# A layer with expert lookup: query weights in sixteen steps of one row, V rows from dot 50, and six places for U from dot 48

## The reference

```python
h = rms_norm(x, norm2_g)
qc = (h @ w_query).reshape(T, 8, 2, 128)              # 8 heads, 2 halves
s = einsum('chpd,hpnd->chpn', qc, sub_keys)           # 128 keys a half
top_s, top_i = top_k(s, 16)                           # of both halves
cand_s, cand_i = all 16 x 16 sums of a pair, and 128 * i0 + i1
best_s, best_pos = top_k(cand_s, 16)                  # 16 experts a head
g = softmax(best_s)
act = gelu(einsum('chkd,cd->chk', expert_u[expert_idx], h))
out = x + einsum('chk,chkd->cd', g * act, expert_v[expert_idx])
```

## Time and profile before

| | |
|---|---|
| median of three runs | 1734.62 us (1733.67 to 1737.07) |
| profiled execution | 1737.77 us, its span 1735.9 us |
| VectorE busy | 1315.3 us, 76% |
| TensorE busy | 1300.8 us, 75% |
| GpSimd busy | 889.8 us, 51% |
| ScalarE busy | 413.4 us, 24% |
| DMA | 584.24 MB, 337 GB/s on average |
| granted TensorE clock | 0.852 of full speed |

### The profile page before, as it was taken

The page is one execution under the profiler, slowest core; times in us unless marked ns, Lnnn a source line. Parts: engine busy times, 40 slices in busy tenths (PEclk is TensorE's granted clock), DMA queues, the critical chain, the costliest instruction groups (busy, mean ns, idle before and its releaser), DMA issues.

```text
span 1735.9 us, 15043 instructions
## 1 busy us (share of the span) xinstructions
PE 1300.8 (75%) x4980; PEld 888.0 (51%) x4980; DVE 1315.3 (76%) x2030; ACT 413.4 (24%) x859; POOL 889.8 (51%) x546
## 2 busy tenths in 40 slices
PE   9999999999984552365556555566597999999950
PEld 7888887778883441122223323333265555555530
DVE  5554655556799999988889999898769665666678
ACT  5333443643110101001034433432054000000000
POOL 1000010000386887888888888888622733334365
PEclk9999999999997776566676788876597999999985
DMA  7886557158799999999999999999965999999998
GB/s 237 220 208 191 173 152 223 59 185 297 267 416 417 421 389 385 382 420 421 414 384 392 393 418 400 391 421 420 394 207 159 403 409 411 409 409 409 409 402 349
DMA packets 150233, 584.24 MB, mean 337 GB/s; under 512 B 15586, under 2 KB 28596, under 8 KB 117268
## 3 DMA queue, kind: packets, MB, share of 16 engines
q0 software_dynamic: 74384, 438.08, 63.2%
q1 hardware_dynamic: 75460, 144.37, 25.2%
q10 hardware_dynamic: 320, 0.93, 0.1%
HBM read 580.95 MB, written 2.36 MB: 336 GB/s over the span
## 4 chain that ended last, share of the span: by engine, by line
POOL 31%; PE 26%; DMA 19%; DVE 16%; issue 7%; ACT 1%; DVEq 0%; ACTq 0%; POOLq 0%
DMA v_rows<-in_peer_expert_v,pick_row 16%; POOL big L676 13%; POOL v_rows L656 11%; POOL more_rows L676 7%; PE ps L1664 6%; PE ps L1666 6%; PE ps L1665 6%; DVE big L1564 4%; DVE more_rows L1522 4%; DVE big L1522 3%; DMA more_rows<-in_peer_expert_u,pick_row 2%; PE ps L2066 1%; PE ps L2090 1%; DVE big L1544 1%; DMA big<-in_peer_expert_u,pick_row 1%
## 5 line engine op out<-in xcount | busy, mean ns | idle before, releaser
L656 POOL DMA_INDIRECT v_rows<-in_peer_expert_v,pick_row x256 | 354.0, 1383 | 292.6 <-DVE big L1564 208.8
L2066 PE MATMUL ps<-v_rows,diag 128*128 128x512 f32 (+1 forms) x480 | 284.8, 749 | 210.4 <-DMA v_rows<-in_peer_expert_v,pick_row 206.1
L1522 DVE CUSTOM_DVE_ANT_0 big<-big 128x2048 f32<-128x2048 f32 x154 | 351.0, 2287 | 45.6 <-DMA big<-in_peer_expert_u,pick_row 45.3
L1564 DVE SCALAR_TENSOR_TENSOR big<-v_rows,pick_w,big 128x1280 f32<-128x1280 f32 x175 | 271.6, 1552 | 130.7 <-DMA v_rows<-in_peer_expert_v,pick_row 126.2
L676 POOL DMA_INDIRECT big<-in_peer_expert_u,pick_row x154 | 299.1, 1942 | 49.2 <-issue 47.2
L2066 PEld LDWEIGHTS ps<-v_rows,diag 128*128 128x128 f32 x480 | 119.3, 265 | 361.9 <-DMA v_rows<-in_peer_expert_v,pick_row 236.0
L1003 DVE TENSOR_TENSOR split_lo<-raw,split_hi 128x1024 fp32r<-128x1024 f32 x119 | 145.8, 1225 | 145.0 <-ACT split_hi L704 119.4
L1522 DVE CUSTOM_DVE_ANT_0 more_rows<-more_rows,big 128x2048 f32<-128x2048 f32 x102 | 232.1, 2286 | 21.5 <-DMA more_rows<-in_peer_expert_u,pick_row 21.1
L676 POOL DMA_INDIRECT more_rows<-in_peer_expert_u,pick_row x102 | 213.2, 2090 | 65.2 <-issue 28.0
L1664 PE MATMUL ps<-split_hi,ht 128*128 128x512 f32 x476 | 189.9, 399 | 1.2 <-DVE split_lo L1053 1.0
L2100 PE MATMUL ps<-big,dense 128*128 128x512 f32 (+1 forms) x512 | 187.5, 489 | 0.7 <-ACT big L931 0.7
(11 more groups left out here) (279 smaller groups left out, 1404.4 us busy)
## 6 DMA issues: line engine op xcount, KB each, us to landing
big<-in_peer_expert_v SPq DMA_DIRECT2D x128, 384.0 KB
raw<-in_w_in SPq DMA_DIRECT2D x88, 512.0 KB, 3.7
raw<-in_w_out SPq DMA_DIRECT2D x32, 512.0 KB, 5.3
big<-in_peer_w_query SPq DMA_DIRECT2D x16, 512.0 KB, 6.6
raw<-in_peer_w_query SPq DMA_DIRECT2D x8, 512.0 KB, 7.7
spare<-in_peer_w_query SPq DMA_DIRECT2D x8, 512.0 KB, 13.1
v_rows<-in_peer_expert_v,pick_row POOLq DMA_INDIRECT x256
big<-in_peer_expert_u,pick_row POOLq DMA_INDIRECT x154, 9.7
```

The source lines that it names most:

```text
L656: pool.indirect_dma_start(v_row(k), None, v_table, bass.IndirectOffsetOnAxis(pick_row[:, k:k + 1], 0)).then_inc(v_gathered[v_place(k)], 16)
L1522: dve.tensor_tensor_reduce(row, row, XN[:, place_of(m // TOPK)[0], :], 1.0, 0.0, ALU.mult, ALU.add, pick_dot[:, m:m + 1]).then_inc(dotted, 1)
L1564: dve.scalar_tensor_tensor(out=v, in0=row, scalar=pick_w[:, k:k + 1], in1=v, op0=ALU.mult, op1=ALU.add).then_inc(added, 1)
L2066: ins = pe.matmul(psf[:, c:c + w], diag[:, k % DIAGS, :], row[:, c:c + w], start=k == 0, stop=k == V_ON_PE - 1)
```

## The change

Three things change. The queries of heads 4 to 7 are made together, in sixteen steps of one row block by 1024 columns into banks 2 to 5, at dots 14, 16, ... 44, and copied out at dot 45 in two copies. V rows are gathered from about dot 50 at 7 for 20 dots, in place of from dot 88 at 3 for 7. U rows go round six places from row 48, in place of row 84. Banks 2 to 5 are also used by V sums (bank 2) and by the first queries, so the first V sum waits for `pq_ready` and the first of the new steps for `pq_first`.

```diff
-              **{32 * c - 50 + 4 * n: (c, n) for c in range(2, W_CHUNKS) for n in range(STEPS_PER_CHUNK)}}
-QUERY_OUT = {12: 1, 43: 2, 75: 3}
+              **{14 + 2 * n: (2, n) for n in range(KC)}}
+QUERY_OUT = {12: 1, 45: 2}
...
-U_WIDE = 84
+U_WIDE = 48
...
-V_FROM, V_BESIDE = 88, 72
+V_FROM, V_BESIDE = 50, 72
...
 def v_until(m):
-    return max(0, m - V_FROM + 1) * 3 // 7
+    return max(0, m - V_FROM + 1) * 7 // 20
...
             def load_query(n):
                 c, q = divmod(n, STEPS_PER_CHUNK)
-                if c:
+                if c > 1:
+                    k = n - 2 * STEPS_PER_CHUNK
+                    src, a = wq_k[:, k:k + 1, 2 * CHUNK:4 * CHUNK], 1
+                elif c:
...
             def query_out(c):
-                act.wait_ge(query_used, (c + 1) * STEPS_PER_CHUNK)
-                act.activation(PQT[:, 4 * c:4 * c + 4, :].rearrange("p w n -> p (w n)"), psf[:, 4 * 512:6 * 512], ACT.Copy).then_inc(sem("pq_ready"), 1)
+                act.wait_ge(query_used, (c + 1) * STEPS_PER_CHUNK if c == 1 else QUERY_STEPS)
+                for f, b in ((1, 4),) if c == 1 else ((2, 2), (3, 4)):
+                    act.activation(PQT[:, 4 * f:4 * f + 4, :].rearrange("p w n -> p (w n)"), psf[:, b * 512:(b + 2) * 512],
+                                   ACT.Copy).then_inc(sem("pq_ready"), 1)
...
                 m = c * STEPS_PER_CHUNK + n
                 query_here(pe, m)
-                if n == 0 and c > 1:
-                    pe.wait_ge(sem("pq_ready"), c - 1)
+                if c > 1:
+                    if n == 0:
+                        pe.wait_ge(sem("pq_ready"), 1)
+                        pe.wait_ge(sem("pq_first"), 3)
+                    for w in range(8):
+                        acc = ps[:, 2 + w // 2, w % 2 * T:(w % 2 + 1) * T]
+                        ins = pe.matmul(acc, query_place(m)[:, w * HD:(w + 1) * HD], x1t[:, n, :], start=n == 0 and w % 2 == 0,
+                                        stop=n == KC - 1, skip_group_check=True)
+                    ins.then_inc(query_used, 1)
+                    return
...
                 if k == 0:
-                    pe.wait_ge(sem("pq_first"), 3)
+                    pe.wait_ge(sem("pq_ready"), 3)
```

## The result

The kernel became slower: 1743.07 us against 1736.34, medians of eight runs each, ratio 1.0038 (95% interval 1.0022 to 1.0055). The forecast was 1725.9 us, 0.5% faster, and the range 1713 to 1741 did not hold it.

A forecast was written before the change was run, and what follows sets the result against it. It took VectorE to bind dots 48 to 87, DMA 88 to 139, gather issue 140 to 235. Terms -1 + 9.4 - 14.7 - 2.4 = -8.7 us, off 1734.6, gave 1725.9 us; range 1713 to 1741.

The forecast's parts named there:

- The wait at row 48: At the change to six places, row 48's gather waits for dot 46; dot 48 starts 5.1 us later (4.0 to 5.8).
- Dots 48 to 139 with V rows: 117.8 MB at the DMA's 421 GB/s take 280 us from the restart; dot 140 comes 9.4 us later, stall included.
- issue binds early: Rival: dots 52 to 139 take 277 us, not 267, limited by gather issue; sum +1.3, 1736 us; chance 0.13.
- check on issue: For 88 dots before dot 140: 20 missing gathers at 1.4 us give 266 us, against DMA's 267, so DMA sets it.
- missing gather: A V gather wanted without a gap of 1.18 us; 1.96 us of waits each in dots 140 to 235, 1.4 earlier.
- Dots 140 to 235: V gathers fall from 42 to 34, missing ones from 14 to 6; 305 us instead of 319.7, 14.7 less.
- slower rival: Dots 140 to 235 gain nothing, DMA and VectorE both needing 3.04 us a dot: +6, 1740.6 us; chance 0.19.
- Dots 236 to 255: The last 20 dots, DMA bound, take 0.12 us less each: 2.4 us less.
- Larger pieces: Query loads in pieces of 4 KB instead of 2 KB take 1 us off dots 0 to 47 (0 to 1.8).
- same bytes in the same DMA-bound stretch: 0: Loads 28 to 31 go out earlier, after steps 16 to 19, at no cost in time.
- Queries late for head 4: Rival: head 4's scores miss dot 48 beyond the stall; up to +5 us, 1731; chance 0.05.
- delay of 0.12 us: GpSimd's release after a two-port VectorE operation, from the Trainium skill; the prediction took 0.88 us from the trace instead.

The follow-up runs named there:

- u48_only: The kernel before with only U_WIDE changed from 84 to 48, so six places from row 48: ratio 1.0040, median 1741.89 us.
- after_order: The changed kernel with the same six places in another order, so that row 48 waits for row 42, not row 46: ratio 1.0004 to the kernel before.
- v_order_spread: The kernel before with the change's V rows, six reordered places from row 48, and search parts in five pairs set apart; old queries: ratio 0.9888, median 1718.17 us.
- after_order_spread: The changed kernel with the six places reordered and a head's search parts done in five pairs set apart: ratio 0.9923 to the kernel before, median 1720.04 us.
- before_spread: The kernel before with a head's ten search parts done in five pairs set apart, V rows and places unchanged: ratio 0.9941, median 1727.77 us.
- after_u36: The changed kernel with U_WIDE = 36, so six places from row 36 instead of row 48: ratio 1.0007 to the kernel before.
- queries_only: The changed kernel with old places and V schedule and one more wait in head_scores, so only the query steps are new: ratio 1.0011 to the kernel before.

## Why the prediction was wrong

- **The wait at row 48**: right, in place, cause and size. 5.1 us was forecast, 5.44 measured, and u48_only and after_order show it alone: 0.34 to 0.40% of the time, about as much as the whole loss. The rest of the change came out near nothing instead of as a gain.
- **Dots 48 to 139 with V rows**: this is the step that failed. "1.4 gives 266. So DMA sets it, narrowly": DMA did not set it. From dot 48 on, 92 dots took 285.2 us where 277.2 had been worked out (dot 140 came 431.4 us after dot 0, not 411.6; 9.4 of the 19.8 were forecast). From the restart at 605.25 to dot 140, 289.6 us passed where the working had 280 to the landing of its row. About 6 us of that are the rate, 412 GB/s and not 421, for the dips shown above and the first slices of the refill. About 3 us are bytes, 119.3 MB and not 117.8: more had landed ahead of dot 140 than was reckoned. With the gaps apart the same stretch took 278.1 us at 419 GB/s (v_order_spread) and 278.3 (after_order_spread), the forecast's number, so issue is what kept the changed kernel from it. The rival "issue binds early" is what happened; at +1.3 us it still fell short of the total.
- **Why the check on issue let it pass**: it set two limits against each other, 266 us for issue and 267 for DMA, and took the larger for the whole stretch. Two limits this close do not give the larger of them: where issue fell behind the rate dipped, and elsewhere DMA was already at 420, so the loss was not made up. The price of a missing gather was nearly right. 30.3 us of waits for 20.5 missing gathers (32 V gathers less 11.5 gaps) are 1.48 each, against the 1.4 taken and the 1.96 of the rival. VectorE's own time was low: 2.71 us a dot has no row, where dots 48 to 87 give 2.76 and this stretch measured (285.2 - 30.3)/92 = 2.77. That alone would not have changed the answer: with 2.76 in both places the working gives a price of 1.23 and 267 us for issue, a tie with DMA again. Nor were dots 88 to 139 of the kernel before, which gave the 1.4, bound by DMA alone: with wider gaps they took 2.8 us less (before_spread).
- **Dots 140 to 235**: right. 305 forecast, 306.8 measured, with 34 V gathers, as said, and waits halved to 12.4 us. In after_u36 the stretch took 312.8 us in its one profiled execution, so the agreement to 2 us is partly luck. The slower rival, which let this stretch gain nothing, did not come; its total (+6) is near the measured one for other reasons.
- **Dots 236 to 255**: 3.9 us less instead of 2.4.
- **Larger pieces**: not the gain that was forecast. -1 us was forecast, the profile has +1.9 in dots 0 to 31, queries_only leans to 0.11% slower, and over eight kernels the difference in these dots is about +1. The step "same bytes in the same DMA-bound stretch: 0" overlooked who gets the bandwidth. U rows get less while the loads run (5.61 MB in 20 us, not 6.53). From about dot 32 VectorE binds (it waits for no row up to dot 45), so bandwidth that the loads leave then is of no use; that this is the cause of the loss is argued. The sentence on the Trainium skill (DMA: Bandwidth & Descriptors, Specifications: full rate from 512 B) was not the question either way, and here 2 KB packets took 13.3% of the engines for a MB in those 20 us, 4 KB packets 12.5.
- **Queries late for head 4**: rightly excluded. The steps took 3.7 us for the most part (0.93 of the clock granted over dots 0 to 45, where the step of 6.5 us had 0.57), and the copies lay at 591.2, 18 us before dot 48 began.
- **The delay of 0.12 us that the prediction took from the Trainium skill** (SBUF — State Buffer; the figure stands there in the section "A bandwidth-pool intuition that's wrong", not in the one named): by it a gap of 0.42 us would do, no gather would be missing, and the pairs would change nothing. The pairs apart gave 0.6 and 1.1%, so the gap that counts is the longer one. But the 0.88 us is not a release delay to set against it: a whole gather takes 0.94 beside an idle VectorE, so the rows show that nearly all of a caught gather comes after the dot's end.

In the profile the terms are +1.9 (dots 0 to 45), +5.6 (46, 47), +12.3 (48 to 139), -12.9 and -3.9, together +3.0 us. The medians say +6.7. The difference of 3.7 us lies within the scatter of single executions, and no stretch was found for it; u48_only shows the same (+2.3 in the profiled one, +5.3 in the medians). The forecast time also started from 1734.6 us, the median of three runs, where the eight runs have 1736.34.

## What to carry to other kernels

When a ring of buffers changes its size on the way, work out for the first rows in the new order which row they wait for: an index that fits at one step can fall two rows back at another, and a new order of the same places removes it. When GpSimd issues gathers beside long VectorE operations, count the gaps of VectorE as a resource of its own, next to bytes and busy time; when two such limits come out within a per cent of each other, expect more than the larger. Lay out the short operations so that the gaps are wide and apart; only then is it worth moving gathers. A load beside a queue that is waited for takes the more of the bandwidth the larger its packets are; what that costs was hardly above the scatter here.

## What the runs showed of the hardware

- Two busy DMA queues sent nearly equal numbers of packets, so bandwidth went with packet size: 8 KB against 2 KB packets moved 6.53 and 1.74 MB in the same 20 us (901 and 898 packets), 8 KB against 4 KB 5.61 and 2.75 (769 and 751).
- A gather caught by a dot ended 0.88 us after the dot, even when the next dot had begun; beside back-to-back dots a gather took 2.0 us on average, beside an idle VectorE 0.94.
- Putting the same short VectorE operations after dots 0, 2, 4, 7 and 9 in pairs, and not singly after ten dots, took 0.6% off the whole kernel, and 1.1% with the V rows spread. Pairs after five dots in a row took nothing (1.0013, 0.9996 to 1.0031).
